# Expert weights read by whole experts instead of halves of a pair of experts

## The reference, cut to what matters

```python
x = x + concat(a_out, b_out, c_out) @ w_out
t = rms_norm(x, norm2)                      # then, over the 16 experts of the layer:
he = silu(t @ w_gate[e]) * (t @ w_up[e])    # w_gate[e], w_up[e]: 1024 x 512
y = y + combine[:, e:e+1] * (he @ w_down[e])  # w_down[e]: 512 x 1024
x = x + y
```

## Time and profile before

| what | us |
|---|---|
| median of 3 runs | 702.59 (701.43 to 703.89) |
| the profiled execution: its time | 701.2 |
| its span | 699.4 |
| TensorE busy | 662.6 (95%) |
| VectorE busy | 298.5 (43%) |
| ScalarE busy | 192.0 (27%) |
| bytes moved by DMA | 240.96 MB, mean 345 GB/s |

### The profile page before, as it was taken

How to read it: one execution, slowest core, us unless ns; L and a number is a source line. 1 busy time by engine, 2 the same in 40 slices (tenths; PEclk the granted TensorE clock), 3 DMA queues, 4 the chain that set the end, 5 groups by cost and what they waited for, 6 DMA issues and landing times.

```text
span 699.4 us, 9145 instructions
## 1 busy us (share of the span) xinstructions
PE 662.6 (95%) x3442; PEld 380.2 (54%) x3442; DVE 298.5 (43%) x632; ACT 192.0 (27%) x342; POOL 16.2 (2%) x29
## 2 busy tenths in 40 slices
PE   6999999999999999997999999999999999999883
PEld 5878778653444444431388878784543353352331
DVE  4478986611232122121474888673221322121234
ACT  3457543421111110100154554342201111111102
POOL 3100000200000000000020000000000000000000
PEclk9999999999999999999999999999999999999998
DMA  9985049999999999999986330998999999999991
GB/s 339 327 291 186 1 189 423 379 412 408 423 420 420 423 420 421 422 421 421 402 291 235 126 121 31 396 422 330 424 419 422 422 420 421 420 422 420 422 408 63
DMA packets 46027, 240.96 MB, mean 345 GB/s; under 512 B 3457, under 2 KB 3649, under 8 KB 21281
## 3 DMA queue, kind: packets, MB, share of 16 engines
q1 hardware_dynamic: 44800, 238.21, 84.2%
q0 software_dynamic: 1040, 2.04, 1.2%
q10 hardware_dynamic: 144, 0.13, 0.1%
HBM read 239.32 MB, written 1.05 MB: 344 GB/s over the span
## 4 chain that ended last, share of the span: by engine, by line
PE 75%; DMA 22%; DVE 1%; issue 1%; ACT 1%; DVEq 0%; SPq 0%
PE psum L1086 23%; PE psum L765 22%; DMA up_w<-in_w_up 21%; PE psum L1119 10%; PE psum L785 4%; PE psum L1066 3%; PE psum L1027 2%; PE psum L745 1%; PE psum L991 1%; PE psum L932 1%; DMA x<-in_x 1%; PE psum L1100 1%; PE psum L844 1%; PE psum L801 1%; PE psum L820 0%
## 5 line engine op out<-in xcount | busy, mean ns | idle before, releaser
L1086 PE MATMUL psum<-up_w,xT 128*64 128x512 f32 x512 | 114.2, 594 | 9.8 <-DMA up_w<-in_w_up 9.8
L1119 PE MATMUL psum<-down_w,scores 128*64 128x512 f32 x512 | 113.5, 595 | 0.0
L765 PE MATMUL psum<-piece_hi,hT_part 128*128 128x512 f32 x320 | 100.1, 394 | 0.0
L1086 PEld LDWEIGHTS psum<-up_w,xT 128*64 128x64 f32 x512 | 36.9, 137 | 83.7 <-issue 64.5
L1119 PEld LDWEIGHTS psum<-down_w,scores 128*64 128x64 f32 x512 | 36.6, 137 | 63.9 <-issue 61.6
L765 PEld LDWEIGHTS psum<-piece_hi,hT_part 128*128 128x128 f32 x320 | 59.0, 188 | 13.2 <-issue 1.7
L1523 DVE TENSOR_TENSOR y_lo<-psum,y_hi 128x512 fp32r<-128x512 f32 x32 | 22.1, 691 | 101.9 <-ACT y_hi L701 101.9
L765 PE MATMUL psum<-piece_lo,hT_part 128*128 128x512 f32 x160 | 62.4, 390 | 0.0
L1086 PE MATMUL psum<-gate_a,xT 128*64 128x512 f32 x256 | 56.9, 594 | 5.0 <-DMA gate_a<-in_w_gate 5.0
L1086 PE MATMUL psum<-gate_b,xT 128*64 128x512 f32 x256 | 56.4, 593 | 0.0
L1502 DVE SCALAR_TENSOR_TENSOR work<-work,psum 128x512 f32<-128x512 f32 x16 | 11.0, 687 | 105.2 <-ACT work L690 105.2
(11 more groups left out here) (243 smaller groups left out, 834.0 us busy)
## 6 DMA issues: line engine op xcount, KB each, us to landing
up_w<-in_w_up SPq DMA_DIRECT2D x32, 2048.0 KB, 17.2
down_w<-in_w_down SPq DMA_DIRECT2D x64, 1024.0 KB, 14.4
gate_b<-in_w_gate SPq DMA_DIRECT2D x32, 1024.0 KB, 14.4
gate_a<-in_w_gate SPq DMA_DIRECT2D x32, 1024.0 KB, 18.3
up_w<-in_w_in SPq DMA_DIRECT2D x6, 2048.0 KB, 13.2
down_w<-in_w_in SPq DMA_DIRECT2D x4, 2048.0 KB, 20.7
down_w<-in_w_out SPq DMA_DIRECT2D x4, 2048.0 KB, 8.1
up_w<-in_w_in SPq DMA_DIRECT2D x4, 1024.0 KB, 8.8
```

The lines of the kernel that those rows point to most:

```text
L765: ins = pe.matmul(o, tokens, w[b][:, c, :], start=(c == 0 and n == 0), stop=(c == DC - 1 and n == len(parts) - 1))
L1086: ins = pe.matmul(psum[e * SLOTS:(e + 1) * SLOTS, bank, :], xT[:, c, k:k + SLOTS], w[:, e, c, :], start=(c == 0), stop=(c == DC - 1))
L1119: ins = pe.matmul(psum[e * SLOTS:(e + 1) * SLOTS, 2 + n, :], heT[:, c, e * SLOTS:(e + 1) * SLOTS], down_w[:, e, c, n * COLS:(n + 1) * COLS ...
```

## The change

The weights of gate, up and down are loaded and used expert by expert: a half is now a whole expert (16 KB in a row for each partition), and PE runs all chunks of expert 0, then all of expert 1. Only in the first gate block of a layer do chunks 0 to 3 still take turns. The second half of expert 1's gate weights ('the tail', 8 KB in a row) of every even item is loaded by itself: for items 0 and 4 into the place of five tables of `const` (`logc`, `decay`, `cos`, `sin`, `swap`: together 8 KB), for items 2 and 6 into `gate_b`. In a layer the tail of item 0 is issued once the retention's decays are made (`decayed`), that of item 2 behind the first weights of all kinds, ahead of `items_ready`. So the tables are loaded again in layer 1, behind the fourth mixing piece; their readers wait for it, and DVE makes `logq` after two splits of weights that it made before them. `final_norm` goes to a place of its own, after the last output projection.

```diff
@@ sync engine: loads
-                def load_halves(dst, src, loaded, used, g, q, back=0, halves=(0, 1), experts=(0, 1)):
-                    for b in halves:
+                def load_experts(dst, src, loaded, used, g, q, back=0, experts=(0, 1), top=DC):
+                    for e in experts:
                         if used is not None:
-                            sp.wait_ge(used.sem, used.at(g, b + 1 - back * used.turn))
+                            sp.wait_ge(used.sem, used.at(g, e + 1 - back * used.turn))
                             settle(sp)
-                        if dst is up_w:
-                            sp.dma_start(dst[:, :, 4 * b:4 * b + 4, :], src[bass.ds(q, 1), :, :, 4 * b:4 * b + 4, :]
-                                         .rearrange("q p e c n -> (q p) e c n")).then_inc(loaded[b].sem, 16)
-                            continue
-                        if dst is down_w:
-                            part = slice(2 * b, 2 * b + 2), slice(None)
-                        else:
-                            part = slice(4 * b, 4 * b + 4), slice(None)
-                        for e in experts:
-                            sp.dma_start(dst[:, e, part[0], part[1]], src[bass.ds(q, 1), :, e, part[0], part[1]]
-                                         .rearrange("q p c n -> (q p) c n")).then_inc(loaded[b].sem, 16)
+                        rows = slice(None) if e == 0 or top == DC else slice(0, top)
+                        sp.dma_start(dst[:, e, rows], src[bass.ds(q, 1), :, e, rows].rearrange("q p c n -> (q p) c n")).then_inc(loaded[e].sem, 16)
+
+                def load_tail(k, q):
+                    sp.dma_start((gate_tail, gate_w[0][:, 1, TAIL:DC])[k], gate_d[bass.ds(q, 1), :, 1, TAIL:DC, :]
+                                 .rearrange("q p c n -> (q p) c n")).then_inc(tail_loaded[k].sem, 16)
...
+                    if l > 0 and j == CQK:
+                        mixing = slice(CONST_AT["logc"][0], CONST_AT["before"][0])
+                        sp.dma_start(const[:, mixing], table[:, mixing]).then_inc(const_loaded.sem, 16)
...
+                sp.wait_ge(decayed.sem, decayed.at(l, 1))
+                settle(sp)
+                load_tail(0, l * PAIRS)
                 sp.wait_ge(projected.sem, projected.at(l, BV + 1))
...
+                load_tail(1, l * PAIRS + 2)
...
+                with sp.Fori(first + 4, last, 4) as g0:
+                    for i in range(4):
+                        load_gate(g0 + i, i % 2)
+                        if i == 0:
+                            load_tail(0, pair(g0))
+                            load_tail(1, pair(g0 + 2))
+                        load_up(g0 + i)
+                        load_down(g0 + i)
@@ tensor engine: gate and up
-                        for c in range(DC):
-                            if bank == 0 and i % 2 == 0:
-                                tokens_ready(pe, g0, i // GROUP, i % GROUP // 2, c)
-                            if c % 4 == 0:
-                                pe.wait_ge(loaded[c // 4].sem, loaded[c // 4].at(turn_of, loaded[0].turn))
-                            for e in range(2):
-                                k = (i % GROUP) * P + e * SLOTS
-                                ins = pe.matmul(psum[e * SLOTS:(e + 1) * SLOTS, bank, :], xT[:, c, k:k + SLOTS],
-                                                w[:, e, c, :], start=(c == 0), stop=(c == DC - 1))
-                            if c % 4 == 3:
-                                ins.then_inc(done.sem, 1)
+                        for e in range(2):
+                            if begun == 0:
+                                pe.wait_ge(loaded[e].sem, loaded[e].at(turn_of, 16))
+                            for c in range(begun, DC):
+                                if bank == 0 and i % 2 == 0 and e == 0:
+                                    tokens_ready(pe, g0, i // GROUP, i % GROUP // 2, c)
+                                ins = hidden(e, c)
+                            ins.then_inc(done.sem, 1)
@@ tensor engine: down
-                            for c in range(2 * b, 2 * b + 2):
-                                for e in range(2):
-                                    ins = pe.matmul(psum[e * SLOTS:(e + 1) * SLOTS, 2 + n, :], heT[:, c, e * SLOTS:(e + 1) * SLOTS],
-                                                    down_w[:, e, c, n * COLS:(n + 1) * COLS], start=(c == 0), stop=(c == HC - 1))
+                            for c in range(HC):
+                                ins = pe.matmul(psum[e * SLOTS:(e + 1) * SLOTS, 2 + n, :], heT[:, c, e * SLOTS:(e + 1) * SLOTS],
+                                                down_w[:, e, c, n * COLS:(n + 1) * COLS], start=(c == 0), stop=(c == HC - 1))
```

More of the change, by code:

```diff
@@ L50 @@
 WARM = 3
+TAIL = DC // 2
 EPS = 1e-6
@@ L200, in hybrid_trunk @@
         pickT = over("pickT", [P, 2, T, P], nc.sbuf_base - 4 * C_W * T)
[L201 to L202 removed]
         sgate = sb("sgate", [P, T, C_W])
         wsT = sb("wsT", [P, 4, P])
[L205 removed]
+        mix_a_lo = over("mix_a_lo", [P, 2, SEQ], nc.sbuf_base - 4 * 4 * P)
         pick = over("pick", [P, T, 2 * GROUP, SLOTS], nc.sbuf_base - 4 * T * GROUP_SLOTS)
+        ws = sb("ws", [P, 4, P])
+        mix_a = [over("mix_a_hi", [P, 2, SEQ], nc.sbuf_base - 4 * 4 * P), mix_a_lo]
         ln_g = sb("ln_g", [P, A_W])
         ln_b = sb("ln_b", [P, A_W])
+        last_gain = nc.alloc_sbuf_tensor_at("last_gain", [P, D], F32, offset=nc.sbuf_base - 4 * D)
         gn_g = sb("gn_g", [P, C_W])
@@ L304, in hybrid_trunk @@
         scales_ready = signal("scales_ready", 1)
-        gate_loaded = [[signal(f"gate_loaded{o}{b}", 32) for b in range(2)] for o in range(2)]
-        up_loaded = [signal(f"up_loaded{b}", 16) for b in range(2)]
-        down_loaded = [signal(f"down_loaded{b}", 32) for b in range(2)]
+        gate_loaded = [[signal(f"gate_loaded{o}{e}", 16) for e in range(2)] for o in range(2)]
+        up_loaded = [signal(f"up_loaded{e}", 16) for e in range(2)]
+        down_loaded = [signal(f"down_loaded{e}", 16) for e in range(2)]
+        tail_loaded = [signal(f"tail_loaded{k}", 16) for k in range(2)]
         gated, upped, gate_tanh = signal("gated", 2, 8), signal("upped", 2, 8), signal("gate_tanh", 1)
@@ L458, in load_gate @@
                 def load_gate(g, o):
-                    load_halves(gate_w[o], gate_d, gate_loaded[o], gated, g, pair(g), 2)
+                    load_experts(gate_w[o], gate_d, gate_loaded[o], gated, g, pair(g), 2, top=TAIL if o == 0 else DC)
                 def load_up(g):
-                    load_halves(up_w, up_d, up_loaded, upped, g, pair(g), 1)
+                    load_experts(up_w, up_d, up_loaded, upped, g, pair(g), 1)
                 def load_down(g):
-                    load_halves(down_w, down_d, down_loaded, downed, g, pair(g), 1)
+                    load_experts(down_w, down_d, down_loaded, downed, g, pair(g), 1)
                 load_gate(first + 2, 0)
@@ L523, in _ @@
                 load_mix_params(l + 1)
-            pool.wait_ge(decayed.sem, decayed.at(DEPTH - 1, 1))
-            pool.dma_start(C("decay"), final_norm.rearrange("(a n) -> a n", a=1).to_broadcast([P, D])).then_inc(final_loaded.sem, 16)
+            pool.wait_ge(out_done.sem, out_done.at(DEPTH - 1, 2 * T))
+            pool.dma_start(last_gain[:], final_norm.rearrange("(a n) -> a n", a=1).to_broadcast([P, D])).then_inc(final_loaded.sem, 16)
         @block.scalar
@@ L1078, in item, with hidden @@
                     for bank, w, loaded, turn_of, done in ((0, gate_w[o], gate_loaded[o], halves, gated), (1, up_w, up_loaded, g0 + i, upped)):
-                        for c in range(DC):
-                            if bank == 0 and i % 2 == 0:
-                                tokens_ready(pe, g0, i // GROUP, i % GROUP // 2, c)
-                            if c % 4 == 0:
-                                pe.wait_ge(loaded[c // 4].sem, loaded[c // 4].at(turn_of, loaded[0].turn))
-                            for e in range(2):
-                                k = (i % GROUP) * P + e * SLOTS
-                                ins = pe.matmul(psum[e * SLOTS:(e + 1) * SLOTS, bank, :], xT[:, c, k:k + SLOTS],
-                                                w[:, e, c, :], start=(c == 0), stop=(c == DC - 1))
-                            if c % 4 == 3:
-                                ins.then_inc(done.sem, 1)
+                        def hidden(e, c):
+                            k = (i % GROUP) * P + e * SLOTS
+                            tail = bank == 0 and i % 2 == 0 and e == 1
+                            if tail and c == TAIL:
+                                arrived = tail_loaded[i % 4 // 2]
+                                pe.wait_ge(arrived.sem, arrived.group(g0, i // 4, 16))
+                            weights = gate_tail[:, c - TAIL, :] if tail and i % 4 == 0 and c >= TAIL else w[:, e, c, :]
+                            return pe.matmul(psum[e * SLOTS:(e + 1) * SLOTS, bank, :], xT[:, c, k:k + SLOTS],
```

(15 more changed lines are left out.)

30 lines of the change are left out of this document (16 added, 14 removed).

## The result

The changed kernel takes 879.43 us (median of 4 runs, 879.23 to 879.64) against 702.72 us (4 runs, 701.43 to 703.89) for the kernel before: ratio 1.2515, 95% interval 1.2493 to 1.2538. It is slower by 176.7 us. The forecast was 712 us with a range of 697 to 750; the result lies outside it, near rival (a) with k = 1 (about 867 us).

A forecast was written before the change was run, and what follows sets the result against it. The prediction took the weight stream and PE as nearly level bounds. Terms of -2.2 + 2.9 + 3.4 + 0.5 = +4.6 us a layer, +9.2 for two, on 701.2 us, with 1.4 for the median, gave 712 us, range 697 to 750.

The forecast's parts named there:

- rival (a): Expert matmuls on PE: each array half holds only k waiting matmuls, so expert 1 starts (7 - k) x 0.858 us late; chance 0.15.
- k = 1: One waiting matmul per array half: 24 blocks x 3.43 us, +82 us a layer, about 867 us in all.
- The step that failed: Expert blocks on PE: each array half works through its own matmuls, passing seven waiting ones, so a block stays 16 steps.
- the terms of the stream: Weight loads in the expert stages: faster packets -2.2, later release +2.9, last landing +3.4 us a layer.
- Rival (b): Expert blocks on PE: no overlap of the experts, matmuls strictly in program order, 30 steps a block, 969 us; chance 0.08.
- Rival (c): Weight stream: not slower, gain balances the 6.8 us a layer lost from 438 GB/s on; 701 us at 440; chance 0.27.
- Rival (d): Weight loads: rows are cut at 8 KB, so packets stay 8 KB; 2.2 us a layer added, 716 us; no chance given.
- The rate term: Weight stream from down of item 1 on: 16 KB packets take 1.3% less time than 8 KB ones, -2.2 us a layer.
- The release term: Weight buffers: both experts finish at block end, so gate 2 and down 1 are issued later; stream 2.9 us late a layer.
- The tail-end term: Last items of a layer: expert 1's whole block stands behind its landing, 6.87 us instead of 3.43, +3.4 us.
- What was costed at nothing: Item 0's tail in the stretch without DMA, tables' second load, moved `logq` (at most 0.5 us either way), `final_norm`: 0 us.

The follow-up runs named there:

- the kernel with the order alone: Kernel before, loads still by halves; PE issues eight matmuls of expert 0, then eight of expert 1, halves released after expert 1: 886.26 us, ratio 1.2622.

## Why the prediction was wrong, point by point

**The step that failed** is "I take it as full, since nothing in the row shows a limit". The L1039 row shows one matmul passed over the earlier trace rows, and the runs show that the limit is close behind: three waiting records, one matmul and a half, where the forecast needed seven matmuls. So expert 1's first record starts 12 steps late (5.15 us) instead of at once. A row that lies wholly inside a limit can't show it. The forecast extended a depth of one to seven, and gave 0.50 to the result of that. Three things follow from the error: PE's work for an item isn't 24.0 us but 36.27; the 14.8 us of waits are gone, as PE is slower than the stream everywhere; and the terms of the stream, which were to make the whole +4.6 us a layer, no longer count.

**Rival (a), k = 1** is the mechanism, and 0.15 was its chance for all k together. Its 867 us were 12 short: it priced 24 blocks at 3.43 us a layer (8 steps of a record each, 192 in all), which leaves out that expert 1 ends alone wherever a stretch ends: 4 steps more, so that a stretch of three loses 28, not 24, and a block that stands alone 12, not 8 (the first gate block, half of it in turns, loses 4). 224 steps in place of 192, twice, are 27.5 us more; against them stand the 14.8 us of waits, which the 867 left in.

**Rival (b)** is out, and so is the rule behind it. (It counts in whole matmuls. Record by record, a strict order gives 7 steps for L1039, not 6, and 31 for a block, not 30; its 969 us would be about 20 higher, and nothing else changes.) The trace shows pairs at each change of expert, and a record that starts ahead of three earlier ones (172.10 before 172.53 to 173.38). The Trainium skill, page "TensorE: Matmul & The Clock Gate", section "Part 3: Packing small matmuls", says that matmuls start and end in strict program order; this trace doesn't agree for two column halves with 512-column float32 records. By the rule runs of 2 matmuls would cost too (expert 1's first record behind three single ones of expert 0), and they measured 1.0006.

**Rival (c)** needed 438 GB/s; the rate with 16 KB rows is 428. **Rival (d)** is out: 34010 packets against 46026 in the kernel with the order alone, and 428 GB/s against 421 once the rows are cut at 8 KB.

**The rate term** (1.3%, 427 GB/s) holds, with 428. **The release term** holds: 2.9 us a layer forecast, 2.9 measured alone, with the issues at 142.15, 149.76 and 161.71 (142.4, 149.96 and 161.9 forecast). That it holds to the tenth is in part luck: the measured kernel has 4 MiB of gate 2 where the forecast had 3. **The tail-end term** (3.4 us a layer) could not be measured as it was meant, since PE never waits for a load after the change, and stays open. The nearest run is turns behind both experts' weights: the three terms give -2.2 + 2.9 + 3.4 = 4.1 us a layer, 8.2 in all, and the profiled execution is 21.8 over. That run waits for more than the forecast's kernel would (expert 0 couldn't start alone), but it shows two costs that no term had: a wait in a middle item (195.70), where the forecast priced only the last one, and 7.4 us of blocks lengthened behind idle stretches. **What was costed at nothing** (the tail in the idle stretch, the tables' second load, `logq`, `final_norm`): those parts together, with whatever the tail's lead gains, measure 0.9989 (0.9977 to 1.0002). That fits; none was measured by itself.

## What to carry to other kernels

Where two halves of the array work side by side, issue them in turns, or in runs of at most two float32 matmuls (of 512 columns, as measured here) for each: longer runs serialise them at a steep price, with no wait in the profile to point to it; the sign is PE's busy time, which rises (114.2 to 196.6 us for the same 512 records) while the mean of a record stays. When a row shows that something works once, ask what length or depth it was shown for, and let the chances follow the shown depth rather than the absence of a limit. And when a wait for data is moved from halves to whole blocks, count the waits in the middle of the stage and the clock behind them, not only the last block.

## What the runs showed of the hardware that was not expected

- Three waiting records of one column half can be passed by a record of the other (12 single starts, then four pairs, at a change of expert after 16 records; 4 single starts with 8 records), and a fourth can't. The depth was seen with 64-column weights and 512-column float32 data only. Whether it counts records or matmuls (two records each), and whether each half holds its own three or the engine looks four ahead in all, these runs don't tell.
- Records of the two halves start out of the order of the code, by up to three.
- Each change of expert after a full half leaves a slip of 57 ns.
- With turns behind whole experts, 2.72 us of idle PE were followed by 2.6 us at a granted clock of 0.50 at 271.10 (the block took 8.68 us), but not at 337.23, behind as long an idle stretch, nor at 603.96, behind 3.69 us (both 7.09 us); what decides between them is open.
